# Copying expert weight chunks from landing to working place on GpSimd instead of VectorE, chunk by chunk

## The chip, the core and the metric

The kernel runs on one NeuronCore of a Trainium2 chip. TensorE does the matmuls, VectorE, ScalarE and GpSimd the elementwise work, SyncE's queue issues most transfers. The metric is device microseconds from the first to the last instruction; three runs of the kernel before gave 1765.09, 1780.57 and 1766.38 us, so the median is 1766.38.

## The reference

One inference step of a one-layer backbone: a token mixer (RWKV-7 scan in both directions beside grouped-query attention) and then a mixture of experts on 384 tokens (128 of a prompt, 256 latent), model width 1024. Only the second part matters here. Cut to its core:

```
logits = h @ w_router + b_router                 # 384 x 32
top_val, top_idx = top_k(logits, 4); gates = softmax(top_val)
for every expert e, for its tokens x:            # w1[e]: 1024 x 2048, w2[e]: 1024 x 1024, float32
    glu, lin = split(x @ w1[e] + b1[e])
    glu = min(glu, 7); lin = clip(lin, -7, 7)
    act = glu * sigmoid(1.702 * glu) * (lin + 1)
    y = act @ w2[e] + b2[e]                      # added to the token's row, times its gate
```

All 32 experts are read: 12 chunks of 1024 KB each, 8 of `w_moe_in` and 4 of `w_moe_out`.

## The kernel before, in words

The token mixer takes the first 700 us or so. Then the router is worked out, and the tokens of each expert are cut into blocks of at most 64. With the inputs at hand that gives 39 blocks for 32 experts: seven experts have two. A table `tab` on the chip holds, for each block, its expert, and each engine has a loop over the blocks (`with gp.Fori(0, last_it) as it`, and likewise on `pe`, `sc`, `ve`), with one more block behind it, the last. SyncE's loop is over experts. What orders the engines is written out by hand: counters (semaphores) that each engine adds to and waits for.

One block `it` on TensorE (L1148 to L1184): biases into banks 0 and 1; for each of the 8 chunks of `w_moe_in` the gate half into bank 0 and the linear half into bank 1. Chunks 0 to 3 are done one by one; of chunks 4 to 7 first all gate halves, after which bank 0 is complete (`gmm`), then the linear halves. After each chunk's linear half `mult` goes up by one: this tells that the chunk's place is no longer read. Then TensorE turns the gathered rows of the next block (`turn_rows`, waits for the gather's `xgd`), turns the activations in two halves (`turn_act`, waits for VectorE's `actd`), and multiplies with the 4 chunks of `w_moe_out`, each again with its `mult`.

VectorE in a block (L1922 to L1930), called the gate chain: a clamp of bank 0 (L1923, the first instruction in each block and the mark by which blocks are told apart here), the product with ScalarE's tanh (L1925, both inputs in SBUF), and when all 8 chunks are done, for each of two halves, a clamp of bank 1 (L1929) and the activation (L1930, both inputs in SBUF).

Where chunks lie: chunks 0 to 6 land in a landing place (`stage[c]`, in the program's names ring, work) and are copied to a working place (`slot[c]`: first, work, spare, zbuf) from which TensorE reads; chunks 7 to 11 have no landing place and land where TensorE reads them. Copies are counted by `stg`. Before, VectorE makes the seven copies for block `it+1` at the end of its part of block `it` (L1933 to L1937): for each chunk it waits until it has landed (`s_es[c]`) and until TensorE has left the working place (`mult`). A second block of the same expert is copied once more from the same landing place.

SyncE issues the 12 chunks of an expert in the order 0 to 11 (`next_expert`, L597 to L603, the transfer itself at L582). Chunks 0 to 6 wait until their landing place was copied for the last time for the expert before (`stg`), chunks 7 to 11 until TensorE's `mult` shows the place free. The queue is in order: a chunk that waits holds all behind it.

GpSimd in the loop (L680 to L683) waits until TensorE has turned the rows of block `it` (`xtm`), and gathers the rows of block `it+1` with an indirect transfer (L660 to L674), with three tiny instructions ahead of it. Its program is in order too.

Of the kernel before, what the change touches and what calls it, by code (L numbers as in the profile page):

```python
# [25 lines left out]
ALU = mybir.AluOpType  # L26
# [3 lines left out]
P = 128  # L30
# [9 lines left out]
NE = 32  # L40
# [26 lines left out]
ZQ_ALL = ZQC * (NZ + 2 * D // CH)  # L67
# [18 lines left out]
WC = W1C + W2C  # L86
NPAIR = 4
W2K = [0, 2, 1, 3]
NST = 7
# [58 lines left out]
def build(nc, a, o):  # L148
    ctx = ExitStack()
    with ctx:  # L150
        sb = lambda n, s, d=F32: ctx.enter_context(nc.sbuf_tensor(n, s, d))
# [22 lines left out]
        condf = sb("condf", [P, 2, 16])  # L174
        condT = sb("condT", [P, KC, 2])
        stat = sb("stat", [P, 64])
        half = sb("half", [P, 16])
        bonus = sb("bonus", [P, NT, 2, HR])
        states = sb("states", [P, 2, 4, HD])
        smallc = sb("smallc", [P, 2, 20])  # L180
# [2 lines left out]
        tab = sb("tab", [1, FIRST_ENDS + 1], I32)  # L183
# [13 lines left out]
        def at(buf, start, *shape, rows=P):  # L197
            n = int(np.prod(shape))
            v = buf[0:rows, start:start + n]
            if len(shape) == 1:  # L200
                return v
            names = "abcd"[:len(shape)]
            return v.rearrange(f"p ({' '.join(names)}) -> p {' '.join(names)}",
                               **{names[i]: shape[i] for i in range(len(shape))})
# [64 lines left out]
        slot = [at(ring, 4 * CW, CW), at(ring, 5 * CW, CW), at(work, 0, CW), at(work, CW, CW)]  # L269
# [6 lines left out]
        stage = slot[0:NST]  # L276
# [66 lines left out]
        S = {n: sem("s_" + n) for n in names}  # L343
# [10 lines left out]
        s_es = [sem(f"s_es{i}") for i in range(WC)]  # L354
# [267 lines left out]
        @block.gpsimd  # L622
        def _(gp):
            gp.memset(at(ky, 0, D), 0.0).then_inc(S["gpn"], 1)
            gp.memset(half[:, :], -0.5).then_inc(S["gpn"], 1)
            gp.wait_ge(S["gpn"], 2)
            rs = ALU.pow
            for j in range(NT):
                gp.wait_ge(S["ssq"], j + 1)
                gp.tensor_tensor(stat[:, 8 + j:9 + j], stat[:, 4 + j:5 + j], half[:, 0:1], rs).then_inc(S["rstd"], 1)  # L630
            for j in range(NT):
                gp.wait_ge(S["anorm"], j + 1)
                gp.tensor_tensor(stat[:, 36:46], stat[:, 26:36], half[:, 0:10], rs).then_inc(S["arstd"], 1)
            for j in range(NT):
                gp.wait_ge(S["kkss"], j + 1)
                gp.tensor_tensor(stat[:, 16:24], stat[:, 8:16], half[:, 0:8], rs).then_inc(S["kkr"], 1)

            def rest_of_bias(i):
                rows = slice((0, 2 * NE)[i], QMAX)
                gp.wait_ge(S["kkr"], NT + i + 2)  # L640
                gp.wait_ge(S["b3d"], (1, 4)[i])
                gp.tensor_tensor(bias32[rows, :], bias32[rows, :], b3[rows, :], ALU.subtract).then_inc(S["b3d"], 1)

            for j in range(NT):
                gp.wait_ge(S["kkss"], NT + j + 1)
                if j == 2:
                    gp.wait_ge(S["b3d"], 2)
                gp.tensor_tensor(stat[:, 16:24], stat[:, 8:16], half[:, 0:8], rs).then_inc(S["kkr"], 1)
                if j:
                    rest_of_bias(j - 1)  # L650
            gp.wait_ge(S["b3d"], 5)
            for j in range(NT):
                gp.wait_ge(S["ssq"], NT + j + 1)
                gp.tensor_tensor(stat[:, 8 + j:9 + j], stat[:, 4 + j:5 + j], half[:, 0:1], rs).then_inc(S["rstd"], 1)

            def gather_rows():
                gp.indirect_dma_start(xg, None, h2_d.rearrange("t (h n) -> (t h) n", h=2), bass.IndirectOffsetOnAxis(ap=slots[:, 0:1], axis=0),
                                      bounds_check=2 * NT * P - 1, oob_is_err=False).then_inc(S["xgd"], 16)

            def gather_first():  # L660
                gp.wait_ge(S["idxc"], 1)
                gp.wait_ge(S["h2out"], 16 * NT)
                gp.tensor_tensor(half[:, 12:13], half[:, 13:14], half[:, 13:14], ALU.mult).then_inc(S["gpn"], 1)
                gather_rows()

            def gather_listed(it):
                gp.wait_ge(S["idxc"], 2)
                gp.wait_ge(S["xgd"], 16 * it + 16)
                gp.wait_ge(S["gpn"], 3 * it + 3)
                gp.tensor_tensor(half[:, 12:13], half[:, 13:14], half[:, 13:14], ALU.mult).then_inc(S["gpn"], 1)  # L670
                gp.tensor_copy(slots[:, 0:1], lists[:, bass.ds(it + 1, 1)]).then_inc(S["gpn"], 1)
                gp.wait_ge(S["gpn"], 3 * it + 5)
                gp.tensor_tensor(half[:, 14:15], half[:, 13:14], half[:, 13:14], ALU.mult).then_inc(S["gpn"], 1)
                gather_rows()  # L674

            gather_first()
            gp.wait_ge(S["routeq"], 12)
            last_it = gp.value_load(tab[0:1, LAST:LAST + 1], min_val=NE - 1, max_val=NBMAX - 1)

            def block_of(it, last):  # L680
                if not last:
                    gp.wait_ge(S["xtm"], it + 1)
                    gather_listed(it)  # L683

            with gp.Fori(0, last_it) as it:
                block_of(it, False)
            block_of(last_it, True)

            gp.wait_ge(S["yo"], 32 * last_it + 32)
            gp.wait_ge(S["gpn"], 3 * last_it + 3)  # L690
            gp.wait_ge(S["stg"], NST * last_it + 2 * NST)
            gp.tensor_tensor(half[:, 12:13], half[:, 13:14], half[:, 13:14], ALU.mult)
            for n in range(NT * TOPK):
                gp.indirect_dma_start(ygat[n], None, rows_d,
                                      bass.IndirectOffsetOnAxis(ap=dest[:, n:n + 1], axis=0))\
                  .then_inc(s_yg[n // TOPK], 16)
            for j in range(NT):
                gp.wait_ge(S["ssq"], 2 * NT + j + 1)
                gp.tensor_tensor(stat[:, 8 + j:9 + j], stat[:, 4 + j:5 + j], half[:, 0:1], rs).then_inc(S["rstd"], 1)
# [736 lines left out]
        def _(ve):  # L1436
            chain = [0, S["chain"]]
            L = lambda ins: link(ve, chain, ins)
            tt, ts, stt, cp = ve.tensor_tensor, ve.tensor_scalar, ve.scalar_tensor_tensor, ve.tensor_copy
# [41 lines left out]
            for i in z_order(lambda t: z_low(ve, t)):  # L1481
                m, j = zunits[i]
                if m < NZ and i % 2:
                    c, n = ZCHUNKS[m]
# [103 lines left out]
            for p, pair in enumerate(pairs):  # L1588
# [24 lines left out]
                for d, j in pair:  # L1613
# [4 lines left out]
                    e, n = 2 * chunk_of(0, d) + 1, 2 * chunk_of(1, d)  # L1618
# [37 lines left out]
                for k in range(2):  # L1656
# [12 lines left out]
                    for d, j in pair:  # L1669
# [7 lines left out]
                        e = 2 * chunk_of(k, d) + 1  # L1677
# [230 lines left out]
            def block_of(it, last):  # L1908
                if last:
                    ve.wait_ge(S["stg"], NST * it + 2 * NST)  # L1910
                    ve.wait_ge(S["xtm"], it + 1)
                    L(tt(lasthot, iota[:, 0:HB].unsqueeze(1).broadcast_to([P, NA, HB]),
                         rel.unsqueeze(2).broadcast_to([P, NA, HB]), ALU.is_equal))
                    L(tt(lasthot, lasthot, gate[:, :, :].rearrange("p j k -> p (j k)").unsqueeze(2).broadcast_to([P, NA, HB]), M))
                    for j in range(NT):
                        for h in range(2):
                            ins = ve.tensor_reduce(onto[:, j, h, :], lasthot[:, TOPK * j:TOPK * (j + 1), :].rearrange("p k t -> p t k"), X, A_)
                    ins.then_inc(S["cmpd"], 1)
                lchain = [0, S["chain2v"]]
                PER = 3  # L1920
                LL = lambda ins: link(ve, lchain, ins, PER * it)
                ve.wait_ge(S["gmm"], it + 1)  # L1922
                ts(gl, B[0], LIMIT, None, ALU.min).then_inc(S["thd"], 1)  # L1923
                ve.wait_ge(S["thd"], 2 * it + 2)
                LL(stt(gg, th, 1.0, gl, A_, M))  # L1925
                ve.wait_ge(S["mult"], WC * it + (8 + ZQ_ALL))
                for i in range(2):
                    seg = slice(i * 2 * P, (i + 1) * 2 * P)
                    LL(ts(uu[:, seg], B[1][:, seg], LIMIT, -LIMIT, ALU.min, ALU.max))  # L1929
                    stt(act[:, seg], uu[:, seg], 1.0, gg[:, seg], A_, M).then_inc(S["actd"], 1)  # L1930
                assert lchain[0] == PER
                if not last:
                    e = ve.value_load(tab[0:1, bass.ds(it + 1, 1)], min_val=0, max_val=NE - 1)  # L1933
                    for c in range(NST):
                        ve.wait_ge(s_es[c], e * 16 + 16)
                        ve.wait_ge(S["mult"], WC * it + (c + 1 + ZQ_ALL))
                        cp(slot[c], stage[c]).then_inc(S["stg"], 1)  # L1937

            with ve.Fori(0, last_it) as it:
                block_of(it, False)  # L1940
# [76 lines left out]
```

## Time and profile before

| what | value |
|---|---|
| runs of the kernel | 1765.09, 1780.57, 1766.38 us, median 1766.38 |
| profiled execution, span | 1789.1 us (one execution of its own; its time is this span, from first to last instruction) |
| TensorE busy, matmul | 1551.3 us, 87% |
| VectorE busy | 845.8 us, 47% |
| ScalarE busy | 262.3 us, 15% |
| GpSimd busy | 125.2 us, 7% |
| mean granted clock of TensorE | 0.911 of full speed |
| read from and written to HBM | 493.12 MB, 22.72 MB |
| chain that ended last | TensorE 60%, transfers 20%, VectorE 11% |
| the seven copies, L1937 | 266 instructions in groups of 38, 1220 to 1228 ns each |

Read it so: the busy shares are of the whole span, in which the mixer and the experts' loop lie one behind the other; which engine sets the pace of the loop is seen only in windows of the loop. TensorE's busy time is modelled from pipelined matmuls. Register, branch and semaphore instructions don't count as busy.

### The profile page before, as it was taken

What the parts mean: (1) busy time and instruction counts of PE and PEld (TensorE: products, weight loads), DVE (VectorE), ACT (ScalarE), POOL (GpSimd) and SP (SyncE); (2) the same over time, 40 slices, a digit from 0 to 9 for tenths busy, and PEclk for the clock granted to TensorE, in tenths of its full rate; (3) what the DMA queues carried; (4) which work ended last, traced back from release to release, by engine and by line L of the source; (5) the groups of instructions that cost most, each with busy time, mean ns of one, the idle gap of its engine ahead of it and who ended that gap; (6) DMA issues with size and microseconds to landing.
All of it is one profiled execution on the core that took longest, in us unless ns stands there. A gap on an engine that the chain in (4) does not pass through costs nothing.

```text
span 1789.1 us, 29229 instructions
## 1 busy us (share of the span) xinstructions
PE 1551.3 (87%) x11144; PEld 759.7 (42%) x11145; DVE 845.8 (47%) x1238; ACT 262.3 (15%) x508; POOL 125.2 (7%) x193
## 2 busy tenths in 40 slices
PE   2699959788989897798997997997998999999893
PEld 0588824467879444232332332332332233233231
DVE  1433253476777636633534443444443443443455
ACT  0223312121130210010110110111101011011100
POOL 0000010000000300100000000000000000000012
PEclk7799965588999898799999999999999999999997
DMA  8624482210000654599999999999999999999995
GB/s 341 212 96 157 171 319 95 77 67 9 3 3 4 216 216 171 226 418 422 353 421 422 372 423 423 358 423 421 375 422 422 390 389 421 395 393 421 385 399 216
DMA packets 98526, 513.00 MB, mean 287 GB/s; under 512 B 14824, under 2 KB 17144, under 8 KB 45752
## 3 DMA queue, kind: packets, MB, share of 16 engines
q1 hardware_dynamic: 81928, 480.88, 66.9%
q10 hardware_dynamic: 11680, 18.49, 2.8%
q0 software_dynamic: 4848, 12.59, 2.0%
q8 instruction: 56, 0.92, 0.2%
q14 instruction: 14, 0.11, 0.0%
HBM read 493.12 MB, written 22.72 MB: 288 GB/s over the span
## 4 chain that ended last, share of the span: by engine, by line
PE 60%; DMA 20%; DVE 11%; SPq 3%; issue 3%; POOL 1%; ACT 1%; DVEq 0%; ACTq 0%; POOLq 0%
PE bank L705 57%; DMA work<-w_moe_in 16%; PE bank L712 3%; SPq L582 3%; DMA ring<-w_ada 1%; DVE work L1929 1%; DMA ring<-rows_d,dest 1%; DVE work L1627 1%; DVE work L1930 1%; DMA work<-mods_d 1%; DMA work<-b_moe_out 1%; DVE work L1636 0%; DVE work L1948 0%; DMA rows_d<-work 0%; DVE work L1720 0%
## 5 line engine op out<-in xcount | busy, mean ns | idle before, releaser
L705 PE MATMUL bank<-work 64*64 64x64 f32 (+4 forms) x5174 | 417.2, 301 | 11.0 <-DVE work L1937 4.1
L705 PE MATMUL bank<-ring,work 128*64 128x512 f32 (+1 forms) x1440 | 363.8, 598 | 10.0 <-ACT work L1204 5.6
L705 PE MATMUL bank<-zbuf,work 128*64 128x512 f32 (+3 forms) x1566 | 291.9, 471 | 57.4 <-DVE zbuf L1937 52.9
L705 PEld LDWEIGHTS bank<-work 64*64 64x64 f32 (+3 forms) x5174 | 224.8, 138 | 182.4 <-issue 144.4
L705 PEld LDWEIGHTS bank<-ring,work 128*64 128x64 f32 (+1 forms) x1440 | 123.4, 145 | 218.1 <-issue 204.1
L705 PEld LDWEIGHTS bank<-zbuf,work 128*64 128x64 f32 (+3 forms) x1566 | 119.0, 151 | 214.7 <-issue 114.8
L1204 ACT ACTIVATE work<-bank 128x512 f32<-128x512 f32 (+2 forms) x226 | 113.0, 513 | 627.6 <-PE bank L705 345.2
L1937 DVE COPY zbuf<-work 128x2048 f32<-128x2048 f32 x114 | 137.0, 1222 | 94.7 <-DMA work<-w_moe_in 92.2
L705 PE MATMUL bank<-parts 128*128 128x512 f32 (+1 forms) x720 | 157.3, 381 | 3.4 <-DVE parts L433 3.4
L712 PE MATMUL bank<-ident,work 128*128 128x128 f32 (+2 forms) x404 | 89.1, 340 | 72.7 <-DVE work L1473 21.7
L705 PEld LDWEIGHTS bank<-parts 128*128 128x128 f32 x720 | 131.1, 190 | 29.7 <-issue 3.4
L1923 DVE TENSOR_SCALAR work<-bank 128x512 f32<-128x512 f32 x39 | 27.0, 692 | 244.9 <-PE bank L705 244.9
L712 PEld LDWEIGHTS bank<-ident,work 128*128 128x128 f32 (+2 forms) x404 | 58.7, 185 | 120.6 <-issue 39.9
L1404 ACT ACTIVATE work<-work 128x512 f32<-128x512 f32 x39 | 24.6, 630 | 521.9 <-DVE work L1923 521.9
L433 DVE TENSOR_TENSOR parts<-ring,parts 128x1024 fp32r<-128x1024 f32 (+1 forms) x40 | 45.7, 1146 | 103.3 <-ACT parts L428 103.3
L705 PE MATMUL bank<-spare,work 128*64 128x512 f32 (+1 forms) x360 | 83.4, 565 | 8.2 <-DVE spare L1937 5.7
L1937 DVE COPY first<-ring 128x2048 f32<-128x2048 f32 x38 | 46.6, 1227 | 80.6 <-DMA ring<-w_moe_in 65.4
L705 PE MATMUL bank<-first,work 128*64 128x512 f32 x312 | 75.5, 604 | 0.3 <-DVE first L1937 0.3
L670 POOL TENSOR_TENSOR half<-half 128x1 f32<-128x1 f32 x38 | 8.0, 211 | 881.2 <-PE bank L712 869.2
L1929 DVE TENSOR_SCALAR work<-bank 128x256 f32<-128x256 f32 x78 | 32.9, 421 | 54.4 <-PE bank L705 54.4
L1937 DVE COPY work<-ring 128x2048 f32<-128x2048 f32 x38 | 46.7, 1228 | 24.2 <-DMA ring<-w_moe_in 20.3
L1937 DVE COPY spare<-work 128x2048 f32<-128x2048 f32 x38 | 46.4, 1220 | 20.8 <-DMA work<-w_moe_in 20.6
(256 smaller groups left out, 1044.8 us busy)
## 6 DMA issues: line engine op xcount, KB each, us to landing
work<-w_moe_in SPq DMA_DIRECT2D x192, 1024.0 KB, 20.5
ring<-w_moe_out SPq DMA_DIRECT2D x128, 1024.0 KB, 16.8
ring<-w_moe_in SPq DMA_DIRECT2D x64, 1024.0 KB, 11.8
ring<-w_ada SPq DMA_DIRECT2D x12, 2048.0 KB, 8.6
ring<-w_in SPq DMA_DIRECT2D x9, 2048.0 KB, 7.9
rows_d<-work ACTq DMA_DIRECT2D x76, 128.0 KB, 7.0
rows_d<-ky SPq DMA_DIRECT2D x11, 512.0 KB, 15.0
ring<-w_out SPq DMA_DIRECT2D x2, 2048.0 KB, 12.5
```

What stands on the lines that cost most here:

```text
L433: eng.tensor_tensor(zpart(t, 1, n), z_quarter(t), zpart(t, 0, n), ALU.subtract)\
L582: sp.dma_start(stage[c] if c < NST else slot[c], src).then_inc(s_es[c], 16)
L670: gp.tensor_tensor(half[:, 12:13], half[:, 13:14], half[:, 13:14], ALU.mult).then_inc(S["gpn"], 1)
L705: return pe.matmul(out, l, r, start=start, stop=stop)
L712: return pe.transpose(out, src, ident[0:n, 0:n])
L1204: cp = lambda out, src, scale=1.0: sc.activation(out, src, ACT.Copy, scale=scale)
L1404: sc.activation(th, gl, ACT.Tanh, scale=ALPHA / 2).then_inc(S["thd"], 1)
L1627: tt(dst, bk(d, 2 * par + i).rearrange("p (c n) -> p c n", c=2), gramm[:, d:d + 1, :].broadcast_to([P, 2, 4 * HC]), M).then_inc(S["am"], 1)
L1923: ts(gl, B[0], LIMIT, None, ALU.min).then_inc(S["thd"], 1)
L1929: LL(ts(uu[:, seg], B[1][:, seg], LIMIT, -LIMIT, ALU.min, ALU.max))
L1930: stt(act[:, seg], uu[:, seg], 1.0, gg[:, seg], A_, M).then_inc(S["actd"], 1)
L1937: cp(slot[c], stage[c]).then_inc(S["stg"], 1)
```

## The change

The seven copies for block `it+1` are taken out of VectorE's program and put into GpSimd's, behind the gather for block `it+1`. The two waits for each chunk are the same. One wait is added ahead of the seven (all copies of the block before are counted), and ahead of each copy stands a multiply of one column into a place of its own in `half`, which is made wider for it. As GpSimd comes to them without the gate chain ahead, a copy may start as soon as its chunk has landed and TensorE has left its place.

```
-        half = sb("half", [P, 16])
+        half = sb("half", [P, 24])
...
                 if not last:
                     gp.wait_ge(S["xtm"], it + 1)
                     gather_listed(it)
+                    e = gp.value_load(tab[0:1, bass.ds(it + 1, 1)], min_val=0, max_val=NE - 1)
+                    gp.wait_ge(S["stg"], NST * it + 2 * NST)
+                    for c in range(NST):
+                        gp.wait_ge(s_es[c], e * 16 + 16)
+                        gp.wait_ge(S["mult"], WC * it + (c + 1 + ZQ_ALL))
+                        gp.tensor_tensor(half[:, 16 + c:17 + c], half[:, 13:14], half[:, 13:14], ALU.mult)
+                        gp.tensor_copy(slot[c], stage[c]).then_inc(S["stg"], 1)
...
                 assert lchain[0] == PER
-                if not last:
-                    e = ve.value_load(tab[0:1, bass.ds(it + 1, 1)], min_val=0, max_val=NE - 1)
-                    for c in range(NST):
-                        ve.wait_ge(s_es[c], e * 16 + 16)
-                        ve.wait_ge(S["mult"], WC * it + (c + 1 + ZQ_ALL))
-                        cp(slot[c], stage[c]).then_inc(S["stg"], 1)
```

## Rows read from the trace of the kernel before

**Rows 1.** Windows of the loop: us, busy us per engine, granted clock, DMA share, GB/s.
```profile
747.90:1738.90 991.00, 913.67 (x4182) 307.57 (x4180) 435.18 (x502) 108.20 (x228) 70.95 (x150) 0.98 0.98 400
985.51:1008.98 23.47, 23.12 (x112) 8.19 (x110) 11.04 (x13) 2.85 (x6) 2.12 (x4) 1.00 0.98 387
1008.98:1032.46 23.48, 23.12 (x112) 8.19 (x110) 11.05 (x14) 2.85 (x6) 2.11 (x4) 1.00 0.94 363
...
1055.93:1085.20 29.27, 24.38 (x112) 7.65 (x110) 11.59 (x14) 2.85 (x6) 1.55 (x4) 1.00 1.01 422
1085.20:1115.94 30.74, 24.80 (x112) 7.48 (x110) 11.58 (x14) 2.85 (x6) 1.55 (x4) 1.00 1.01 421
```

**Rows 2.** Chain of waits that ended last, in the loop: start us, us, what.
```profile
1038.13 21.21 PE bank L705 x100
1059.49 24.53 DMA work<-w_moe_in
```

**Rows 3.** Waits of SyncE's queue: waiter, releaser, us in total, times, longest.
```profile
SPq L582 <- DVE first L1937: 151.5, 7, 22.5
```

**Rows 4.** Timeline of SyncE's queue, 985 to 1030 us: start us, us, what.
```profile
992.51 1.47 SPq L582 DMA_DIRECT2D ring<-w_moe_in  x2
994.77 18.11 SPq L582 DMA_DIRECT2D work<-w_moe_in  x6
1016.70 5.59 SPq L582 DMA_DIRECT2D ring<-w_moe_out  x4
1024.25 0.92 SPq L582 DMA_DIRECT2D ring<-w_moe_in  x2
```

**Rows 5.** The page's costliest groups: busy us, mean ns of one, idle before, releaser.
```profile
L1937 DVE COPY zbuf<-work 128x2048 f32<-128x2048 f32 x114 | 137.0, 1222 | 94.7 <-DMA work<-w_moe_in 92.2
```

**Rows 6.** Timeline of VectorE, 950 to 1070 us: start us, us, what, [idle before].
```profile
981.96 1.23 DVE L1937 COPY zbuf<-work 128x2048 f32<-128x2048 f32 x1 [1.25 <-DMA work<-w_moe_in]
...
1032.46 0.69 DVE L1923 TENSOR_SCALAR work<-bank 128x512 f32<-128x512 f32 x1 [9.84 <-PE bank L705]
1033.84 0.69 DVE L1925 SCALAR_TENSOR_TENSOR work<-work 128x512 f32<-128x512 f32 x1 [0.70 <-ACT work L1404]
...
1036.35 0.42 DVE L1930 SCALAR_TENSOR_TENSOR work<-work 128x256 f32<-128x256 f32 x1
...
1037.14 0.42 DVE L1930 SCALAR_TENSOR_TENSOR work<-work 128x256 f32<-128x256 f32 x1
...
1041.85 1.23 DVE L1937 COPY spare<-work 128x2048 f32<-128x2048 f32 x1 [0.30 <-DMA work<-w_moe_in]
```

**Rows 7.** Timeline of TensorE, 1000 to 1040 us, same columns.
```profile
1021.94 1.89 PE L705 MATMUL bank<-first,work 128*64 128x512 f32 x8
...
1032.24 2.75 PE L705 MATMUL bank<-zbuf,work 128*64 128x512 f32 x12
...
1037.62 0.51 PE L712 MATMUL bank<-ident,work 128*128 128x128 f32 x2 [0.29 <-DVE work L1930]
1038.06 2.37 PE L705 MATMUL bank<-ring,work 128*64 128x512 f32 x10
```

**Rows 8.** Groups of GpSimd's instructions, shapes apart, columns as rows 5.
```profile
L624 POOL MEMSET ky<- 128x1024 f32 x1 | 1.0, 951 | 0.3 <-POOLq L2005 0.3
```

**Rows 9.** Timelines of VectorE and of GpSimd, 600 to 630 us.
```profile
601.34 0.69 DVE L1720 TENSOR_TENSOR work<-work,stat 128x512 f32<-128x512 f32 x1 [0.99 <-POOL stat L648]
...
622.10 5.99 POOL L642 TENSOR_TENSOR work<-work,rowc 32x3072 f32<-32x3072 f32 x1
...
622.12 6.52 DVE L1720 TENSOR_TENSOR work<-work,stat 128x512 f32<-128x512 f32 x1 [1.00 <-POOL stat L648]
```

**Rows 10.** Timeline of GpSimd, the gather of one block.
```profile
1013.23 0.18 POOL L670 TENSOR_TENSOR half<-half 128x1 f32<-128x1 f32 x1 [20.77 <-PE bank L712]
...
1014.31 1.61 POOL L657 DMA_INDIRECT zbuf<-h_d,slots  x1 [0.50 <-issue]
```

**Rows 11.** What uses the tile `slots`: the 39 gathers, from issue to landing.
```profile
DMA to landing us min/median/max: 3.3/6.7/8.1
```

## The prediction, made before the changed kernel was run

> **What bounds the kernel now.** I read the windows first, one per expert block, cut at the first VectorE instruction of each block's gate chain (the clamp of bank 0). The loop over 39 blocks takes 991 of the 1789.1 us and moves 400 GB/s on average; a block whose weights came in time takes 23.47 us, of which TensorE is busy 23.12, and one that waits for weights takes 29.27 to 30.74 us at 421 to 422 GB/s [rows 1]. So two limits alternate, and the chain of waits says the same: 21.21 us of TensorE per block, then 24.53 us of weight transfer [rows 2]. 32 experts are loaded but 39 blocks run: seven experts have two blocks, and after each the period falls to 23.5 us for about three blocks, until the transfers are behind again.
>
> The transfers lose time only around those seven: 387 and 363 GB/s in the first two periods after the first block of such an expert (call it D, then D'), against 422 [rows 1]. That is (422-387)/422 x 23.47 = 1.9 us and (422-363)/422 x 23.48 = 3.3 us, 5.2 us each time, 36 us in seven. The queue of SyncE shows why. Its seven waits for the copy into `first`, 151.5 us in all, are the wait for landing place 0 [rows 3]: in D the places are held until the second block's copies. It issues chunks 0 to 6 from 992.51 on, chunk 7 at 1012.55 (the last of the six of 994.77: start plus 18.11, less its 0.33), the four of w_moe_out from 1016.70 and the next expert from 1024.25 [rows 4]. An expert's 12 chunks of 1024 KB are 12.58 MB, at 421 GB/s [rows 1] 29.9 us or 2.49 us a chunk, so seven need 17.4 us; started at 992.5 with some 2 us before data flow, they are in by 1012. Chunk 7 isn't held by a copy but by TensorE, which must be through with all eight chunks of w_moe_in of D'.
>
> **What the change moves.** *VectorE's side.* Seven copies of 1.22 us [rows 5] leave it per block, 8.6 us. They stood behind the gate chain, in the time in which TensorE works on w_moe_out. Nobody behind them on VectorE waits: the next clamp comes when TensorE is ready, so this gives 0.
>
> *Earlier release.* GpSimd may copy chunk c when TensorE has left chunk c of the running block, for chunks 0 to 3 up to 8.6 us ahead of the clamp (1021.94 plus 1.72 plus 0.2 against 1032.46) and for 4 to 6 at 0.8, 1.7 and 2.5 us behind it (chunk 4's last matmul ends at 1032.24 + 0.86) [rows 6, 7]. In an ordinary block SyncE comes to place 0 only at 1024.25 [rows 4], 15.3 us after the clamp at 1008.98; copies that start 5.6 us after it and take 8.5 are over by then, so nothing is gained. In D it would be let on about 3.8 us earlier (below). But then seven chunks are in by 1008 and chunk 7 still waits for TensorE: the idle time of the transfers moves from before the seven chunks to behind them. I take 0; the ends are 0 and the whole 36 us.
>
> *What a copy costs on GpSimd.* The trace has no such copy. Nearest from below is its memset, 0.951 us for 1024 columns, one stream [rows 8]; with some 0.1 us of start, twice the columns are 1.8 us. From above, its subtract of two inputs, 5.99 us for 3072 columns [rows 9], by two thirds 4.0 us. A copy reads one stream and writes one, and these can overlap, so I take 1.9, near the memset, and keep both ends. With the tiny multiply ahead of each (0.18 us, starts 0.13 apart in the gather [rows 10]) that is 2.05 us, under the landing pace of 2.49: GpSimd keeps up. Per block it works 7 x 2.05 + 2.7 (gather: 1013.23 to 1015.92 [rows 10]) = 17 us, within 23.5.
> The Trainium skill (GPSIMD Engine Reference, section 3.1) gives two figures for one-input work: 1.03 cycles per element for bodies of at most two operations, and 1.8 cycles as the best case of an unrolled loop. By the first a copy of 2048 is 1.76 us and the sum below stands; by the second it is 3.07 us, which would be the slow-copy rival. No row settles it.
>
> *The collision.* At 620 us the trace shows both engines at once: a VectorE tensor_tensor of 512 columns with both inputs in SBUF, elsewhere 0.69 us, takes 6.52 us when GpSimd's subtract started 0.02 us ahead of it, and ends 0.55 us behind that [rows 9]. It stood still for the whole GpSimd instruction. In the loop VectorE has three such instructions per block on TensorE's path: the product at 1033.84 and the two activations at 1036.35 and 1037.14 [rows 6]; the clamps read PSUM. TensorE's transposes wait for the last and w_moe_out begins at 1038.06, 5.60 us after the clamp [rows 7].
> In a block whose next weights have landed, count from the clamp: copy 4 runs 1.0 to 2.9; the product, ready at 1.4, ends at 2.9 + 0.55 = 3.45 instead of 2.07; copy 5 runs 3.6 to 5.5; the first activation, ready at 3.96, ends at 5.8 instead of 4.3; copy 6 runs 5.95 to 7.85; the second ends at 8.15 instead of 5.1. **Plus 3.05 us**, and w_moe_out starts that much later. In the block after D', the copies meet landings (chunk 3 at 1041.85, so chunk 0 near 1034.4 [rows 6]) and only the second activation meets one: about 1.7 us. When transfers lag, chunk 6 lands 3.55 us before the next clamp (below) and chunk 0 six paces earlier, 18.5 before it, which in a period of 29.27 us is 10.8 us behind the last clamp: no collision.
>
> *The moved wait.* In program order the gather for the block after next's rows now stands behind seven copies. In D, chunk 6 lands 3.55 us before the clamp (981.96 against 985.51 [rows 6]); its copy ends at -1.5, the gather is issued 1.08 us later (1013.23 to 1014.31 [rows 10]) at -0.4 and lands 6.7 us after that [rows 11], at 6.3, while TensorE is ready to turn its rows at 3.3. Plus 3.0 us. Behind it, GpSimd's copies for D' run from 0.7 on (place 0 free at 2.8, against 6.7 now for the issue at 992.51: the 3.8 us above) and hold the second activation until 8.0; this lies beside the late gather, so together 3.0, not 6. Chunk 6's slower copy adds 0.4 to D's clamp. In the other lagging blocks TensorE catches up while chunks land every 2.49 us and it needs 1.72 for each: 0. The index copy and value load on GpSimd (0.5 us) stand in idle time.
>
> **Sum.** In D and D' nothing covers a delay, since chunks 8 to 11 are issued as TensorE frees their places [rows 4]: 3.0 + 0.4 + 3.05 = 6.45 us, and from there all transfers run as much later; seven times is 45 us. In the two blocks after them the transfers have work in hand (the eleven chunks issued from 1016.70 on last to about 1046, and the next place 7 is free at 1036), so their 1.7 to 3 us are hidden; if that cover were gone, 7 x 3 = 21 us more. The start (block 0, same situation) adds 3.05, the last block but one 1.7. Together 50 us: the profiled execution goes from 1789.1 to 1839, and the median of the runs, which stands 22.7 us under the profiled span, from 1766.4 to **1816 us**.
>
> **Rivals.**
> *Slow copies.* If a copy costs 3.0 us, between the two bounds, GpSimd is the pace-setter: the three VectorE instructions each wait for most of a copy, the second activation ends near 12 us after the clamp, 7 more than now, and every period is about 30.5 us whether weights are there or not. A group of five blocks takes 5 x 30.6 = 153 us where it takes 130.4 now (985.51 to 1115.94), seven times 22.6 and some 7 at the ends: 165, so 1931 us. At 4.0 us a block needs 7 x 4.15 + 2.7 + the VectorE parts between, 34 us, and the time is 1766 + 38 x 34 - 991 = about 2067. For it: the two-input row; against: the memset row.
> *No collision inside the loop.* If VectorE finds its turn in the gaps, only the late gather and the 0.4 remain: 7 x 3.4 = 24 us, 1790; with gathers that land in 3.3 us [rows 11], nearly nothing, 1768. For it: only one long overlap is in the trace. Against: in that one the lock was complete.
> *Faster.* The mechanism is the early release of place 0 in the seven D blocks. It decides if what holds the transfers there is this release, and not chunk 7 behind TensorE; then 5.2 us come back each time and the time is 1766 - 36 = 1730. For it: 151.5 us of waiting on that copy [rows 3]. Against: 1016.70 and the three issues behind it wait for TensorE, and no place is free in between [rows 4].
> *The copies are no earlier in effect.* Where transfers lag, a copy starts on landing whoever makes it, and elsewhere GpSimd is as late as VectorE was: 1766.
>
> **How the numbers follow.** Collision with quick copies 0.55 (its own range 1790 to 1850); slow copies 0.22, most of it near 3 us; no collision 0.12; faster 0.06; no effect 0.05. The range 1780 to 1940 holds the first, the third from its middle up and the slow case to 3 us, some 0.8. About 1% (1749 to 1784) is what a measurement of this kernel tells from no change; that takes half of the third and the last: 0.11. Faster 0.06, slower 0.83.
>
> **What would show it.** Copies of GpSimd near 1.9 us, 266 of them. VectorE's product and activations longer than 0.69 and 0.42 us, by 1 to 2 us, in periods of 26.5 us where they were 23.5. TensorE waiting for the activations, and in D for the gathered rows. SyncE's wait for place 0 shorter, now on GpSimd, but no higher GB/s: in D' under the 363 of now. I am wrong if the VectorE instructions keep their lengths, if D' moves more bytes per us, or if a copy takes far from 1.9 us.

## The result, and the profile after

The changed kernel takes 1888.52 us (median of 4 runs, 1884.97 to 1897.21), the kernel before 1772.14 (4 runs): a ratio of 1.066, 95% interval 1.059 to 1.072. Slower, as forecast, but by 116 us and not by 50. Ratios here and below leave out executions in a slower state at a lower clock, so they can differ a little from the ratio of the medians.

The profiled execution spans 1883.2 us. What lies ahead of the loop differs between profiled executions by some 24 us (first clamp at 747.9 before, at 724.1 after), so I compare the loop itself, from first to last clamp: 991.0 before, 1839.67 - 724.13 = 1115.5 after.

The same five blocks as in [rows 1], cut at the clamps; the first is D, the second D'. Columns as there: us, busy us per engine, granted clock, DMA share, GB/s.

```profile
980.43:1017.59 37.16, 25.81 (x112) 8.65 (x110) 15.47 (x6) 2.85 (x6) 23.91 (x27) 0.82 0.73 295
1017.59:1045.43 27.84, 24.81 (x112) 8.56 (x110) 6.88 (x6) 2.85 (x6) 8.29 (x10) 0.94 0.65 250
1045.43:1073.17 27.74, 24.60 (x112) 8.35 (x110) 6.92 (x6) 2.85 (x6) 15.64 (x18) 0.94 1.01 424
1073.17:1102.66 29.49, 25.81 (x112) 8.60 (x110) 6.32 (x6) 2.85 (x6) 15.64 (x18) 0.88 1.02 422
1102.66:1127.33 24.67, 23.34 (x112) 8.10 (x110) 3.00 (x6) 2.85 (x6) 15.54 (x18) 1.00 1.02 422
```

These five blocks take 146.9 us where they took 130.4. Nearly all of it is in D (37.16 for 23.47) and D' (27.84 for 23.48); of the three behind them some 1.6 us come back (81.9 for 83.5), as the transfers have had more time. Transfers stand idle in D and D' for 11 + 11 us, (422-295)/422 x 37.16 and (422-250)/422 x 27.84, where it was 5.2.

VectorE in D and D' (start us, us, what): the two-input instructions that answer to [rows 6].

```profile
980.43 0.69 DVE L1930 TENSOR_SCALAR work<-bank 128x512 f32<-128x512 f32 x1 [19.52 <-PE bank L712]
981.82 13.17 DVE L1932 SCALAR_TENSOR_TENSOR work<-work 128x512 f32<-128x512 f32 x1 [0.70 <-ACT work L1411]
...
996.38 0.42 DVE L1937 SCALAR_TENSOR_TENSOR work<-work 128x256 f32<-128x256 f32 x1
1017.59 0.69 DVE L1930 TENSOR_SCALAR work<-bank 128x512 f32<-128x512 f32 x1 [20.79 <-PE bank L712]
1018.98 2.08 DVE L1932 SCALAR_TENSOR_TENSOR work<-work 128x512 f32<-128x512 f32 x1 [0.70 <-ACT work L1411]
...
1021.66 1.56 DVE L1937 SCALAR_TENSOR_TENSOR work<-work 128x256 f32<-128x256 f32 x1
...
1023.59 1.79 DVE L1937 SCALAR_TENSOR_TENSOR work<-work 128x256 f32<-128x256 f32 x1
```

In D the product, 0.69 us of work, takes 13.17. It does so in three of the seven D blocks (13.17 to 13.18). In the other four it takes 11.43 to 11.44: there the first copy began 1.5 us before the clamp, and here 0.25 us behind it. In all seven the product ends 0.55 us behind the end of the seventh copy. What GpSimd does meanwhile, first and last of seven copies without a gap, and what follows them:

```profile
980.68 1.90 POOL L690 COPY first<-ring 128x2048 f32<-128x2048 f32 x1
982.54 0.19 POOL L689 TENSOR_TENSOR half<-half 128x1 f32<-128x1 f32 x1
...
992.57 1.88 POOL L690 COPY zbuf<-work 128x2048 f32<-128x2048 f32 x1
994.42 0.63 POOL L670 TENSOR_TENSOR half<-half 128x1 f32<-128x1 f32 x1
```

The product ends at 994.99, 0.54 us behind the end of the seventh copy at 994.45, just as in [rows 9], and only then GpSimd's next tiny multiply gets through (0.63 us instead of 0.18). A copy takes 1.88 to 1.90 us.

TensorE in D, D' (timeline): the first matmuls of w_moe_out and the bias that ends them, which answer to the 1038.06 of [rows 7].

```profile
985.98 0.65 PE L719 MATMUL bank<-ident,zbuf 128*128 128x128 f32 x4 [2.16 <-DMA zbuf<-h_d,slots]
996.07 1.49 PE L719 MATMUL bank<-ident,work 128*128 128x128 f32 x4 [9.10 <-DVE work L1937]
997.49 9.31 PE L712 MATMUL bank<-ring,work 128*64 128x512 f32 x32
1006.64 0.60 PE L712 MATMUL bank<-rowc 96*64 96x512 bf16 x4
...
1025.87 8.78 PE L712 MATMUL bank<-ring,work 128*64 128x512 f32 x32
1034.48 0.60 PE L712 MATMUL bank<-rowc 96*64 96x512 bf16 x4
```

w_moe_out begins 17.06 us after the clamp in D and 8.28 in D', for 5.60 before: 11.46 and 2.68 us more. And it takes longer: 9.15 and 8.61 us. Windows of just these stretches, two of after and two of before (same columns as above):

```profile
986.00:997.49 11.49, 2.30 (x10) 1.14 (x10) 10.61 (x5) 0.98 (x2) 10.40 (x13) 0.60 1.01 422
997.49:1006.64 9.15, 9.15 (x33) 2.85 (x34) 0.00 (x0) 0.64 (x2) 0.00 (x0) 0.75 0.94 387
1025.87:1034.48 8.61, 8.61 (x33) 2.72 (x34) 0.00 (x0) 0.64 (x2) 1.04 (x1) 0.80 0.48 171
```

```profile
1014.59:1021.50 6.91, 6.91 (x33) 2.32 (x34) 6.91 (x7) 0.64 (x2) 1.33 (x1) 1.00 0.90 324
1038.06:1044.97 6.91, 6.91 (x33) 2.32 (x34) 5.16 (x5) 0.64 (x2) 1.34 (x1) 1.00 1.01 419
```

The same 32 matmuls and the first of the bias take 6.91 us at full clock; behind these stalls TensorE's granted clock is at 0.5, the lower of its two levels (1.2 GHz instead of 2.4), for the first part of them, and they take 2.24 us more in D, 1.70 in D'. The sum closes: 11.46 + 2.24 = 13.7 is D's 37.16 - 23.47, and 2.68 + 1.70 = 4.4 is 27.84 - 23.48 in D'. Over the whole loop the seven D periods take 86.2 us more than before (34.66 to 37.21 us each) and the seven D' periods 30, of 124.5 us in all.

The wait of SyncE's queue for landing place 0, 151.5 us in [rows 3], did shrink, but the queue waits longer for TensorE. In the loop, before and after (us in total, times, longest):

```profile
SPq L582 <- PE bank L705: 418.1, 151, 14.5
```

```profile
SPq L582 <- PE bank L712: 646.4, 150, 26.0
SPq L582 <- POOL first L690: 94.9, 7, 15.5
```

### The profile page after: what moved, and what is told of

The parts are those of the page before. It is cut to its first block, busy times and chain, and to the rows that moved or that the text cites. A ratio compares the mean times of both kernels' runs of the same rounds, so it can differ in the third digit from the quotient of the medians.

```text
span 1883.2 us, 29533 instructions
## 1 busy us (share of the span) xinstructions
PE 1566.8 (83%) x11144; PEld 760.4 (40%) x11145; DVE 686.8 (36%) x971; ACT 260.0 (14%) x508; POOL 654.9 (35%) x726
## 4 chain that ended last, share of the span: by engine, by line
PE 54%; DVE 19%; DMA 16%; issue 5%; SPq 2%; POOL 2%; ACT 1%; DVEq 0%; ACTq 0%; POOLq 0%
PE bank L712 52%; DMA work<-w_moe_in 12%; DVE work L1932 6%; PE bank L719 3%; DVE work L1937 3%; SPq L582 1%; DVE work L1936 1%; DMA ring<-w_ada 1%; POOL zbuf L690 1%; DVE work L1634 1%; DMA work<-mods_d 1%; DVE work L1930 1%; ACT work L1411 1%; DMA work<-b_moe_out 1%; DMA ring<-rows_d,dest 0%
## 5 line engine op out<-in xcount | busy, mean ns | idle before, releaser
L712 PE MATMUL bank<-ring,work 128*64 128x512 f32 (+1 forms) x1440 | 415.8, 679 | 7.7 <-ACT work L1211 5.4
L712 PE MATMUL bank<-work 64*64 64x64 f32 (+4 forms) x5174 | 402.0, 297 | 6.6 <-DVE work L1899 2.7
L712 PE MATMUL bank<-zbuf,work 128*64 128x512 f32 (+3 forms) x1566 | 278.4, 459 | 23.3 <-POOL zbuf L690 19.1
L719 PE MATMUL bank<-ident,work 128*128 128x128 f32 (+2 forms) x404 | 88.2, 341 | 192.5 <-DVE work L1937 131.2
L712 PEld LDWEIGHTS bank<-ring,work 128*64 128x64 f32 (+1 forms) x1440 | 135.0, 164 | 260.8 <-issue 250.1
L689 POOL TENSOR_TENSOR half<-half 128x1 f32<-128x1 f32 x266 | 55.6, 209 | 490.5 <-DMA ring<-w_moe_in 324.3
L690 POOL COPY zbuf<-work 128x2048 f32<-128x2048 f32 x114 | 215.1, 1887 | 0.0
L1932 DVE SCALAR_TENSOR_TENSOR work<-work 128x512 f32<-128x512 f32 x39 | 127.6, 3272 | 27.2 <-ACT work L1411 26.5
L1937 DVE SCALAR_TENSOR_TENSOR work<-work 128x256 f32<-128x256 f32 x78 | 91.1, 1168 | 2.7
L648 POOL TENSOR_TENSOR stat<-stat,half 128x8 f32<-128x8 f32 x3 | 4.9, 1640 | 243.6 <-DVE stat L1723 243.6
L633 POOL TENSOR_TENSOR stat<-stat,half 128x10 f32<-128x10 f32 x3 | 5.9, 1957 | 210.1 <-DVE stat L1506 210.1
```

What stands on the lines that cost most here:

```text
L689: gp.tensor_tensor(half[:, 16 + c:17 + c], half[:, 13:14], half[:, 13:14], ALU.mult)
L690: gp.tensor_copy(slot[c], stage[c]).then_inc(S["stg"], 1)
L712: return pe.matmul(out, l, r, start=start, stop=stop)
L719: return pe.transpose(out, src, ident[0:n, 0:n])
```

## The experiments

Each edits the kernel before or the changed one in one place or two. Ratios are to the kernel before, run on the same chip with them, with their 95% interval. Next to them stands what the one trace of each shows: the loop from first to last clamp, and the seven D periods together.

| kernel | ratio (95% interval) | loop, us | seven D, us |
|---|---|---|---|
| before | | 991.0 | 165.0 |
| changed | 1.066 (1.059 to 1.072) | 1115.5 | 251.2 |
| e1 | 1.034 (1.027 to 1.041) | 1051.6 | 187.8 |
| e2 | 1.003 (0.999 to 1.007) | 1004.8 | 172.2 |
| e3 | 1.000 (0.996 to 1.004) | 998.9 | 178.0 |
| e4 | 1.010 (1.004 to 1.017) | 1003.4 | 179.1 |
| e5 | one run, none | 1073.2 | 211.9 |
| e6 | 1.014 (1.005 to 1.022) | 1008.2 | 183.0 |
| e7 | 1.011 (1.003 to 1.019) | 1015.9 | 167.3 |
| e8 | 1.022 (1.013 to 1.030) | 1020.0 | 189.8 |
| e9 | 1.027 (1.022 to 1.033) | 1045.9 | 192.5 |
| e10 | 1.017 (1.013 to 1.022) | 1021.1 | 184.2 |

**e1, one copy issued at a time.** Edit of the changed kernel (`mult` line shown for its place):

```
                         gp.wait_ge(S["mult"], WC * it + (c + 1 + ZQ_ALL))
+                        gp.wait_ge(S["stg"], NST * it + (2 * NST + c))
```

> The changed kernel, with one more wait ahead of each copy on GpSimd: the copy before it must be complete. So never more than one copy is issued to GpSimd at a time. Theory A (VectorE's two-input instruction waits for every GpSimd instruction that is issued already, so in the first block of a two-block expert for all seven copies): the product there takes 2.1 us at most instead of 13.2 or 11.4, w_moe_out starts 8 to 9 us after the clamp instead of 17, and seven times about 8.5 us come back: 1820 to 1840 us. Theory B (the time in these blocks is lost to the late gather or to slow copies, the long product being only beside it): 1880 to 1895 us as the changed kernel.

Measured: 1833.15 us, ratio 1.034 (1.027 to 1.041). The D product in this trace:

```profile
980.69 1.31 DVE L1933 SCALAR_TENSOR_TENSOR work<-work 128x512 f32<-128x512 f32 x1 [0.70 <-ACT work L1412]
```

It takes 1.31 us for 13.17, and 0.83 to 1.71 in the seven D blocks; w_moe_out begins 7.0 to 8.1 us behind the clamp. Of the 64 us by which the loop is shorter than in the changed kernel, the seven D periods hold 63. Theory A holds and B falls: about half of the loss is that VectorE was held for the whole run of copies.

**e2, copies behind the gate chain.** Edit of the changed kernel:

```
                     gp.wait_ge(S["stg"], NST * it + 2 * NST)
+                    gp.wait_ge(S["actd"], 2 * it + 2)
```

> The changed kernel, but GpSimd begins its copies only when VectorE is through with the block's two activations, so at the point where VectorE made them. No two-input instruction of VectorE meets a copy. Theory A (the collision is the whole loss but for the late gather): periods of 23.5 us again where weights are there, 2 to 3 us per two-block expert left for the gather: 1772 plus 15 to 25, so 1785 to 1800 us. Theory C (copies of 1.9 us in place of 1.2 are too slow for TensorE): more than 1830 us, with TensorE waiting for copies.

Measured: 1784.48 us, ratio 1.003 (0.999 to 1.007), median of 10 runs. The product's group is back at 0.69 us:

```profile
L1933 DVE SCALAR_TENSOR_TENSOR work<-work 128x512 f32<-128x512 f32 x39 | 27.0, 692 | 27.2 <-ACT work L1412 27.2
```

By the times, slow copies and the late gather together are worth no more than 0.7% (theory C falls). In the one trace the loop is 13.8 us longer than before, a little above that.

**e3, the late gather alone.** Edit of the kernel before:

```
                     gp.wait_ge(S["xtm"], it + 1)
+                    gp.wait_ge(S["stg"], NST * it + 2 * NST)
                     gather_listed(it)
```

> The kernel before (copies on VectorE), with one wait more: GpSimd gathers the next block's rows only when all copies for the running block are made, as in the changed kernel. This is the late gather alone. If it costs what the prediction took (3.0 us in each of seven blocks): 1790 to 1795 us. By the trace of the changed kernel, where the rows were turned 5.6 us after the clamp instead of 3.3, less: about 15 us, 1785. If VectorE's chain covers it: 1772, no change.

Measured: 1776.31 us, ratio 1.000 (0.996 to 1.004). TensorE in a D block whose clamp is at 966.78:

```profile
971.23 0.66 PE L713 MATMUL bank<-ident,zbuf 128*128 128x128 f32 x4 [0.68 <-DMA zbuf<-h_d,slots]
```

The rows are turned 4.45 us after the clamp here, 1.1 later than the 3.3 of before, not 3.0; in the seven D blocks they are 0.6 to 2.6 later. The D periods are 0.2 to 5.2 us longer than before, 13 us in all, while the whole loop is 7.9 us longer. So in the trace the late gather alone costs some 1 to 2 us per two-block expert; the times don't resolve it.

**e4, split copies.** GpSimd makes 0 to 3, VectorE 4 to 6. Edit of e1, with the old loop on VectorE for the rest:

```
-                    for c in range(NST):
+                    for c in range(4):
...
+                    for c in range(4, NST):
+                        ve.wait_ge(s_es[c], e * 16 + 16)
+                        ve.wait_ge(S["mult"], WC * it + (c + 1 + ZQ_ALL))
+                        ve.wait_ge(S["stg"], NST * it + (2 * NST + c))
+                        cp(slot[c], stage[c]).then_inc(S["stg"], 1)
```

> GpSimd copies chunks 0 to 3 (each only when the one before is complete), VectorE chunks 4 to 6 behind its gate chain as before. Where weights are there, GpSimd's four copies are over before the clamp, so only the first block of a two-block expert has a collision, of one or two copies, 1 to 2.5 us; the gather is early again. Landing place 0 is free about 6 us earlier there. If the earlier release is worth nothing, as predicted: 1770 to 1795 us. If it gives back the 5.2 us of idle transfers each time: 1735 to 1760 us.

Measured: 1790.67 us, ratio 1.010 (1.004 to 1.017). D and D' in windows:

```profile
960.83:987.42 26.59, 24.59 (x112) 8.33 (x110) 8.60 (x9) 2.85 (x6) 19.03 (x18) 0.94 0.98 407
987.42:1010.89 23.47, 23.11 (x112) 8.16 (x110) 6.67 (x9) 2.85 (x6) 2.19 (x4) 1.00 0.78 287
```

SyncE waits 88.4 us for place 0 instead of 151.5. D moves 407 GB/s instead of the 387 of [rows 1], but D' 287 instead of 363: the idle time has moved behind the seven chunks, and is 0.9 + 7.5 = 8.4 us instead of 5.2, and D is 3.1 us longer. The earlier release gives nothing back that the time or the loop shows.

**e5, one break in the run** (one run). Edit of the changed kernel:

```
+                        if c == 3:
+                            gp.wait_ge(S["stg"], NST * it + (2 * NST + c))
```

> The changed kernel with a single wait in the run of seven copies: copy 3 is issued only when copy 2 is complete. Theory A (the instructions of GpSimd that are issued when VectorE's comes go first, however many): in the first block of a two-block expert the product ends behind copy 2, after about 5 us instead of 13 or 11; whether the first activation, which comes while copies 3 to 6 are issued, then waits for all four (about 7 us) or for one tells if the number issued matters by itself. If all is handed over after the break: about 1833 us as with a wait ahead of every copy; if the activation waits for four: some 5 us more in each of seven blocks, 1865. Theory D (VectorE gets in only when GpSimd has nothing left that could run): the product takes 11 to 13 us as before, 1888 us.

Measured: 1854.67 us in its one run. Product and first activation in a D block, and the third and fourth copy of GpSimd:

```profile
986.56 5.26 DVE L1934 SCALAR_TENSOR_TENSOR work<-work 128x512 f32<-128x512 f32 x1 [0.70 <-ACT work L1413]
...
992.40 1.57 DVE L1939 SCALAR_TENSOR_TENSOR work<-work 128x256 f32<-128x256 f32 x1
```

```profile
989.38 1.88 POOL L692 COPY work<-work 128x2048 f32<-128x2048 f32 x1
991.34 0.52 POOL L691 TENSOR_TENSOR half<-half 128x1 f32<-128x1 f32 x1
991.81 1.89 POOL L692 COPY spare<-work 128x2048 f32<-128x2048 f32 x1
993.66 0.36 POOL L691 TENSOR_TENSOR half<-half 128x1 f32<-128x1 f32 x1
```

The product ends at 991.82, behind copy 2 and the break: theory D falls. It takes 5.26 us in three D blocks and 3.5 in the four where the copies begin ahead of the clamp. But the first activation then waits for copy 3 alone, although copies 4 to 6 could have been issued behind it. The time of the single run lies between the two forecasts.

**e6, the gather between copies 3 and 4.** One copy at a time; the loop of GpSimd becomes

```
+            with gp.Fori(1, last_it) as it:
+                gp.wait_ge(S["xtm"], it + 1)
+                gather_listed(it)
+                copies(it, bass.ds(it, 1), range(4, NST))
+                copies(it + 1, bass.ds(it + 1, 1), range(4))
```

> GpSimd makes all seven copies, one issued at a time, but the gather of the next rows stands between the copies of chunks 3 and 4 (it waits for TensorE's turn, 4 us behind the clamp), so the gather isn't late and copies 4 to 6 come behind most of VectorE's chain. Where weights are there, 0 to 1 us of collision instead of 2.7; in the first block of a two-block expert one to three short waits, 2 to 4 us with the lower clock that follows. Theory A: 1785 to 1805 us. If slow copies matter by themselves: over 1815.

Measured: 1789.48 us, ratio 1.014 (1.005 to 1.022). As theory A.

**e7, a later release.** Edit of the kernel before, SyncE's queue:

```
-                        sp.wait_ge(S["stg"], used * NST + (c + 1))
+                        sp.wait_ge(S["stg"], used * NST + NST)
```

> The kernel before, with one edit in SyncE's queue: a chunk's landing place counts as free only when all seven copies are made, so place 0 is given up about 7 us later in the first block of a two-block expert; elsewhere the queue has work in hand. If the release of place 0 isn't what holds the transfers when it comes earlier (as predicted) they still have to be through with seven chunks before chunk 7's place opens, so later it costs: 7 us less some 3.4 us of idle time that goes, 3 to 5 us in each of seven, 1795 to 1810 us. If the moment of the release counts one for one, both ways: 7 x 7 = 49, 1823. If it doesn't count at all: 1774.

Measured: 1785.36 us, ratio 1.011 (1.003 to 1.019). D and D' in windows:

```profile
956.05:979.80 23.75, 23.40 (x112) 8.18 (x110) 11.03 (x14) 2.85 (x6) 2.11 (x4) 0.99 0.67 258
979.80:1003.26 23.46, 23.11 (x112) 8.19 (x110) 11.03 (x13) 2.85 (x6) 2.10 (x4) 1.00 1.02 424
```

258 and 424 GB/s for 387 and 363: 9.2 us idle, all ahead of the seven chunks, 4.0 more than before. Some 7 us later cost 1.1%, 14 us by the medians and 19 by the ratio, 2 to 3 per two-block expert; from one D to the next the trace has 133.7 us on average for 130.3, 3.4 more. The time lies under the 1795 to 1810 that were forecast, and far from one for one. With e4 it shows both sides: in the kernel before, place 0 is freed early enough that an earlier release brings nothing, and a later one costs.

**e8, copies 4 to 6 behind the chain.** Edit of e1:

```
+                        if c == 4:
+                            gp.wait_ge(S["actd"], 2 * it + 2)
```

> The changed kernel with one copy issued at a time, and chunks 4 to 6 copied only behind the block's second activation. Chunks 0 to 3 are copied early as in the changed kernel. Collisions remain in the first block of a two-block expert alone (up to three, each at most one copy, 3 to 5 us with the lower clock behind) and where chunks 0 to 2 land during the chain; the gather is late there as well, which cost nothing measurable. Theory A: 1785 to 1805 us, against 1833 with copies 4 to 6 free to start; the difference is the price of the collision in blocks whose weights are there.

Measured: 1804.39 us, ratio 1.022 (1.013 to 1.030), at the upper end. Between the ratios of e1 and e8 lie 1.2%, some 21 us: what copies 4 to 6 cost where they are free to meet the chain. 2.2% remain although copies 4 to 6 come behind the chain; product and activations still average 1.00 and 0.98 us, as copies 0 to 3 still meet them in some blocks, and in a D block (clamp at 962.82) the next clamp comes 27.08 us later.

**e9 and e10, a plain delay.** Edit of the kernel before, no copy on GpSimd; 4 reductions in e9, 2 in e10:

```
                 ve.wait_ge(S["mult"], WC * it + (8 + ZQ_ALL))
+                for i in range(4):
+                    ve.tensor_reduce(gl[:, i:i + 1], th, X, A_)
```

> The kernel before (all copies on VectorE, none on GpSimd) with four useless VectorE reductions of 512 columns ahead of the two activations in every block, about 2.6 us, the length of the collision in a block whose weights are there. Theory A (what the collision costs outside the first block of a two-block expert is a stall of TensorE of that length and the low clock behind it, nothing of GpSimd): periods of 27.5 to 28 us where they were 23.5, of which some 1.7 us are TensorE at half clock behind the stall; the time comes near the 1833 us of the spaced copies: 1825 to 1845. If the clock stays up: periods of 26.1, and 1805 to 1815 us.

> The same with two reductions, about 1.3 us. Theory A: half the stall; periods of 24.8 us if the clock stays up behind it, 26 to 26.5 if it falls as well. With two blocks per two-block expert that nothing covers: 7 x 2 x 1.3 = 18 us and the start, 1795 us with the clock up; about 1815 with the clock falling.

Measured: 1815.09 us, ratio 1.027 (1.022 to 1.033), and 1796.48, 1.017 (1.013 to 1.022). VectorE and TensorE in e9:

```profile
1020.79 0.69 DVE L1923 TENSOR_SCALAR work<-bank 128x512 f32<-128x512 f32 x1 [11.31 <-PE bank L705]
...
1024.22 2.46 DVE L1928 TENSOR_REDUCE work<-work 128x1 f32<-128x512 f32 x4 [1.35 <-PE bank L705]
...
1048.10 0.69 DVE L1923 TENSOR_SCALAR work<-bank 128x512 f32<-128x512 f32 x1 [10.89 <-PE bank L705]
```

```profile
1028.33 0.70 PE L712 MATMUL bank<-ident,work 128*128 128x128 f32 x2 [0.29 <-DVE work L1932]
1028.96 8.35 PE L705 MATMUL bank<-ring,work 128*64 128x512 f32 x32
```

and the w_moe_out stretch of two neighbouring blocks in e10:

```profile
1027.57 7.09 PE L705 MATMUL bank<-ring,work 128*64 128x512 f32 x32
...
1052.23 8.78 PE L705 MATMUL bank<-ring,work 128*64 128x512 f32 x32
```

In e9 TensorE stands still for 2.4 us in each block, w_moe_out begins 2.6 us later, and 35 of the 38 periods take 27.2 to 27.6 us: 23.47, the 2.6, and 1.3 us of matmuls at the lower clock. In e10 it stands still for 1.2 us, and a period is 24.65 us (13 of 38) with the granted clock at 1.00 in these matmuls, or 26.35 (14 of 38) with 0.80 and 1.7 us more. So a stall made by VectorE's own work does what GpSimd's copies did, clock included. The times fit less well than the periods. 1815.09 is under theory A's 1825 to 1845 and at the upper end of the forecast with the clock up; 1796.48 is near the 1795 forecast for a clock that stays up, though it fell in a part of the blocks. From one D to the next e9 takes 137.2 us on average in the trace and e1 137.3, so the plain delay accounts for the price of e1 in the loop; why their ratios still differ, 1.027 and 1.034, is open.

## Why the prediction was right and wrong

*VectorE gains nothing by being relieved: right.* With the copies gone from it and no collision (e2), the time is that of before within 0.7%.

*A copy of 1.9 us: right*, 1.88 to 1.90. By the Trainium skill's two figures (GPSIMD Engine Reference, section 3.1), the one of 1.03 cycles per element, 1.76 us, an estimate, is near; the trace speaks against 3.07. The slow-copy rival falls: e2 has the same copies.

*Earlier release worth nothing: right.* Shown by e4 (idle time moves from D to D'), while e7 shows that it counts when later.

*The collision where weights are there: mechanism right, one term missing.* w_moe_out was to begin 8.65 us after the clamp and begins at 8.28: plus 2.68, forecast 3.05. But behind these stalls TensorE also works at its lower clock, 1.70 us more in D', 2.24 in D. I had read the clock column, 1.00 in every single block of [rows 1], and not asked what an idle TensorE would do to it, though slices at lower clock were on the page. The cover behind D' held: the next block takes 27.74 us for 23.47, but the transfers run at 422 to 424 GB/s there and the three blocks together take no longer than before.

*The late gather: wrong, small.* The sum had 3.0 in D. In the changed kernel the rows are turned 5.55 us after the clamp (985.98), 2.25 late, and the held product covers that. Alone, with VectorE's shorter copies ahead of it, the turn is 0.6 to 2.6 us late in the trace, and nothing is measurable in the time (e3).

*D itself: this is the step that failed.* The prediction had GpSimd's copies "hold the second activation until 8.0", beside the late gather: it let VectorE in after the one copy that it met. In D all seven copies are ready at once, and the product, ready 1.4 us after the clamp, ended 14.6 us after it (994.99 against 980.43). The stall is 11.46 us instead of 3.0, and 9.1 to 9.7 in the four D blocks where the copies begin earlier. e1 shows, and the single run of e5 agrees, that the run without a break is the cause. [Rows 9] had one GpSimd instruction, from which one cannot tell whether the port (the access to SBUF that the two engines take from each other) is handed over between two; I took it as given, and this unknown had no upper bound in the sum. With seven copies, 14 us, as its upper bound, the range would have been reasoned from there.

*The sum.* For the five blocks shown: 6.45 forecast, 16.5 measured = 11.46 + 2.24 (D) + 2.68 + 1.70 (D') - 1.6 (behind). From one D to the next it is 15.6 on average, as four of the seven D blocks lose 2 to 3 us less. D and D' together hold 116 of the 124.5 us of the loop. The difference of 10 us in the five blocks shown: 8.5 for D's hold (11.46 for 3.0), 3.9 for the clock, less 0.4 for D', 0.4 for chunk 6's slower copy and 1.6 that came back behind. That the time fell inside the range is owed to the slow-copy rival, which is not what happened.

*Open.* What decides that all seven go first. GpSimd's sequencer works out the threshold of chunk 5's wait at 981.3 and of chunk 6's at 982.2, about when the product is ready (981.82), so most copies were issued ahead of it. But "what is issued goes first" isn't enough: in D' at 1021.66 and in e5 at 992.40 an activation came while the next copies could go, and waited for one copy only. In both VectorE had had the port a moment before. It may be that a run which nothing has broken is kept whole; that is argued, not shown.

No version beat the kernel before: the time gives no sign that early copies are of use here.

## What to carry to other kernels

Before an elementwise job goes to GpSimd, list VectorE's instructions with two SBUF inputs that can meet it, and price each by the longest run of GpSimd instructions that can be ready at once, not by one; a wait on the predecessor's completion ahead of each costs some 0.12 us a copy (starts 2.10 us apart in e1 for 1.98) and took the hold from 13 us to at most 1.7 in the same blocks. Price a stall of TensorE with the matmuls behind it at the lower clock. And an earlier release of a buffer is worth only what the next gate in the same queue leaves of it.

## What the runs showed of the hardware

- A two-input VectorE instruction was held by seven back-to-back GpSimd copies for 13.17 us, ending 0.54 us behind the last; in the one run with a wait in the middle it got in there (5.26 us). The Trainium skill (SBUF — State Buffer, section on the two separate sides) says that a VectorE instruction with two SBUF inputs and a GpSimd instruction that reads SBUF share a pair of ports, that whichever starts first has the pair for the whole instruction, and that the other fully blocks. The trace agrees for one instruction (2.08 us for 0.69 in D'), and goes beyond it: in D it was the whole run.
- A stall of TensorE of 1.2 us was followed by 32 matmuls at full clock (granted clock 1.00, 7.09 us) in one block and partly at the lower level in the next (0.80, 8.78 us). One of 2.4 us was followed by 8.35 us with the lower level in the block shown, and 35 of 38 periods of that kernel have its length.
- A GpSimd copy of 128 x 2048 float32 takes 1.88 to 1.90 us, with or without VectorE beside it, 266 of 266.
